# Starting place of the high weight copies in four buffers: 128, 0, 512 and 144 bytes modulo 1024

## The reference, cut to what matters

```
def _swiglu(xn, w_gate, w_up, w_down):
    return (jax.nn.silu(xn @ w_gate) * (xn @ w_up)) @ w_down
...
h = xn @ w_in                     # conv mixer, 1024 x 3072, then @ w_out
qkv = xn @ w_qkv                  # attention, 1024 x 3072, then @ w_o
proj = h @ w_in                   # second stack's mixer, 1024 x 3600, then @ w_out
```

## Time and profile before

| what | value |
|---|---|
| median of three runs | 2063.25 us |
| profiled execution, first to last instruction | 2062.1 us |
| TensorE matmul busy | 2036.8 us (99%), 9974 records |
| TensorE weight load busy | 1704.7 us (83%) |
| VectorE busy | 1684.8 us (82%) |
| ScalarE busy | 1022.3 us (50%) |
| GpSimd busy | 112.4 us (5%) |
| mean granted TensorE clock | 0.999 of 2.4 GHz |

### The profile page before, as it was taken

How to read it: one execution, slowest core, us unless ns; L and a number is a source line. 1 busy time by engine, 2 the same in 40 slices (tenths; PEclk the granted TensorE clock), 3 DMA queues, 4 the chain that set the end, 5 groups by cost and what they waited for, 6 DMA issues and landing times.

```text
span 2062.1 us, 26087 instructions
## 1 busy us (share of the span) xinstructions
PE 2036.8 (99%) x9974; PEld 1704.7 (83%) x9974; DVE 1684.8 (82%) x2820; ACT 1022.3 (50%) x1216; POOL 112.4 (5%) x238
## 2 busy tenths in 40 slices
PE   8999999999999999999999999999999999999998
PEld 7888878888978888888888889788888888988887
DVE  6888888886579887888889886989888877788986
ACT  4554445444554444554454445765445444575442
POOL 0010010000010000000010000010001000001000
PEclk9999999999999999999999999999999999999999
DMA  8576655756446556565566656346656756535662
GB/s 272 176 237 228 196 173 197 219 196 207 149 144 216 192 184 204 184 214 194 192 212 215 195 183 203 115 154 216 200 185 210 227 188 194 181 112 185 193 195 91
DMA packets 291166, 393.22 MB, mean 191 GB/s; under 512 B 9941, under 2 KB 257061, under 8 KB 290914
## 3 DMA queue, kind: packets, MB, share of 16 engines
q1 hardware_dynamic: 284176, 368.16, 55.1%
q10 hardware_dynamic: 4034, 14.23, 2.1%
q0 software_dynamic: 2832, 9.17, 1.6%
HBM read 390.44 MB, written 2.12 MB: 190 GB/s over the span
## 4 chain that ended last, share of the span: by engine, by line
PE 90%; DVE 6%; ACT 1%; issue 1%; POOL 1%; DMA 0%; POOLq 0%; SPq 0%; ACTq 0%; DVEq 0%
PE psum L577 25%; PE psum L578 25%; PE psum L579 25%; PE psum L601 4%; PE psum L619 2%; PE psum L616 2%; PE psum L623 2%; PE psum L603 2%; DVE w_lo L1569 2%; PE psum L712 1%; DVE conv_tmp L1657 1%; ACT squares L1210 1%; DVE mqk L1657 1%; DVE Y L1596 0%; DVE X L2072 0%
## 5 line engine op out<-in xcount | busy, mean ns | idle before, releaser
L1569 DVE TENSOR_TENSOR w_lo<-raw,w_hi 128x2048 fp32r<-128x2048 f32 x349 | 794.7, 2289 | 137.6 <-ACT w_hi L1184 134.7
L1184 ACT ACTIVATE w_hi<-raw 128x2048 fp32r<-128x2048 f32 x349 | 662.9, 1909 | 115.5 <-PE psum L579 83.3
L577 PE MATMUL psum<-w_hi,xT 128*128 128x512 f32 (+1 forms) x1424 | 552.3, 388 | 1.0 <-DVE xT L1754 1.0
L579 PE MATMUL psum<-w_hi,xT 128*128 128x512 f32 (+1 forms) x1424 | 549.0, 386 | 0.0
L578 PE MATMUL psum<-w_lo,xT 128*128 128x512 f32 (+1 forms) x1424 | 549.0, 386 | 0.0
L1620 DVE STREAM_TRANSPOSE h_turned<-h_full 32x128 f32<-32x128 f32 x1408 | 426.2, 303 | 21.1
L577 PEld LDWEIGHTS psum<-w_hi,xT 128*128 128x128 f32 x1424 | 267.4, 188 | 57.7 <-issue 2.9
L579 PEld LDWEIGHTS psum<-w_hi,xT 128*128 128x128 f32 x1424 | 267.4, 188 | 53.7
L578 PEld LDWEIGHTS psum<-w_lo,xT 128*128 128x128 f32 x1424 | 267.4, 188 | 53.3
L577 PE MATMUL psum<-w_hi,h_hi 128*128 128x512 f32 x768 | 299.5, 390 | 0.0
L579 PE MATMUL psum<-w_hi,h_lo 128*128 128x512 f32 x768 | 298.9, 389 | 0.0
(11 more groups left out here) (241 smaller groups left out, 1958.5 us busy)
## 6 DMA issues: line engine op xcount, KB each, us to landing
raw<-in_ffn_w_in SPq DMA_DIRECT2D x176, 512.0 KB, 4.9
raw<-in_ffn_w_gate SPq DMA_DIRECT2D x88, 512.0 KB, 4.0
raw<-in_ffn_w_up SPq DMA_DIRECT2D x88, 512.0 KB, 5.0
raw<-in_ffn_w_down SPq DMA_DIRECT2D x44, 1024.0 KB, 4.9
raw<-in_ffn_w_out SPq DMA_DIRECT2D x44, 1024.0 KB, 4.9
raw<-in_conv_w_in SPq DMA_DIRECT2D x20, 1024.0 KB, 5.6
raw<-in_mix_w_in SPq DMA_DIRECT2D x16, 1024.0 KB, 5.3
raw<-in_mix_w_in SPq DMA_DIRECT2D x24, 512.0 KB, 4.8
```

The costliest lines, as they stand in the source:

```text
L577: pe.matmul(dst, l_hi, r_hi, start=first, stop=False, skip_group_check=loose)
L579: return pe.matmul(dst, l_lo, r_hi, start=False, stop=last, skip_group_check=loose)
L1184: return act.activation(dst, source, ACT.Copy, **kw)
L1569: dve.tensor_tensor(w_lo[u % LO_RING][:], raw[u % LO_RING][:], f32(high(u)), ALU.subtract).then_inc(lo_ready, 1)
```

## The change

`high(u)` takes its offset from the buffer alone. The offsets are 0, 224, 96 and 4 elements, that is 0, 896, 384 and 16 bytes, so that every unit in buffers 0, 1, 2 and 3 begins at 128, 0, 512 and 144 bytes modulo 1024. The fifth buffer keeps 128. The plan of shifted units goes. No instruction, wait, transfer or buffer is added, removed or moved.

```diff
-ASIDE = 16
-NARROW = {"conv": (2, 3, 4, 5, 6, 7, 8, 9, 10, 12), "attn": tuple(range(2, 12)), "mix": tuple(range(2, 10)), "pool": (0,)}
+ASIDE = (0, 224, 96, 4)
...
-def plan_narrow(stages):
-
-    return {st["u0"] + n for st in stages for n in NARROW.get(st["kind"], ())}
...
-    narrow = plan_narrow(stages)
...
         def high(u):
-            off = ASIDE if hi_slot[u] < HI_RING and u in narrow else 0
+            off = ASIDE[hi_slot[u]] if hi_slot[u] < HI_RING else 0
             return w_hi[hi_slot[u]][:, off:off + UNIT]
```

## The result

The changed kernel takes 2080.01 us (median of four runs, 2079.72 to 2080.31), the kernel before in the same comparison 2063.09 us (2062.82 to 2063.88). The ratio is 1.008, with a 95% interval of 1.0068 to 1.0093: it is slower by 16.9 us. The profiled execution spans 2078.5 us (2062.1 before), at a mean granted clock of 0.998 of 2.4 GHz (0.999 before), so the clock is not the cause; a run of the changed kernel at 1.000 takes 2079.72 us.

The account below looks back on a forecast made before the run. TensorE matmul, busy 99%, was taken as the bound, so time is the sum of distances between its starts. 2062.1 + 13.6 + 0.8 = 2076.5 us, plus 1.15 to the median: 2077.7, given as 2077; 8 in 10: 2056 to 2096.

Parts of the forecast that it names:

- part 1: Long units in buffers 1, 2 and 3: 2960 steps with high weights moving leave their floor by 4.6 ns each, +13.6 us.
- the case of better places: Rival: the new places part two reads that meet in short and wide steps, -5.6 us, 2058 us; chance 0.16.
- restart row: Eight long steps after a restart in the earlier trace, 0.2313 us each, 4.6 ns above the floor; taken as the price.
- the wide row: A 512-column pass in a wide unit, 14 ns above the floor; upper bound for long steps, +41 us.
- Part 2: Short units: seven in buffer 0 go from 192 to 128, +0.8 us; nineteen in the other buffers taken as 0.
- Part 3: Wide units: 15 shifted ones, 16 pairs each, no order by address, taken as 0; bounds -3.4 and +3.4 us.
- Part 4: ScalarE and VectorE touching the high part at its new place: taken as 0; 3.2 us if VectorE slowed 2% without cover.
- The floor holds: Rival: long steps stay at 0.2267 us, as a 512-column step could hide any hold-up of the load; 2064 us, chance 0.34.
- only the 16-byte start hurts: Rival: only buffer 3's 976 matmuls lose 4.6 ns each, +4.5 us; 2069 us, chance 0.06, counted on the forecast's side.

Follow-up runs that it names:

- e1_long: Against the kernel before, only the 302 long units take the new places; the 41 shifted short and wide units stay at 192: 2079.21 us, ratio 1.0076.
- m2_small: Against the kernel before, high weights of long units begin 4, 16, 32 and 48 bytes past 128 in buffers 0 to 3: 2096.19 us, ratio 1.016.
- e2_short: Against the kernel before, only the 41 shifted short and wide units take the new places; long units stay at 128: 2063.51 us, ratio 1.0001.
- e7_buffer1: Against the kernel before, only long units in buffer 1 move, from 128 to 0: 2069.28 us, ratio 1.0027.
- e5_streams: Against the kernel before, all weights begin at 128, xT and h tiles at 256 (out_hi at 512), no unit shifted: 2102.51 us, ratio 1.019.
- e4_no_shift: Against the kernel before, no unit is shifted, all high parts begin at 128: 2065.31 us, ratio 1.001.
- e8_buffer3: Against the kernel before, only long units in buffer 3 move, from 128 to 144: 2071.52 us, ratio 1.0039.

## Why the prediction was right, step by step

The forecast of 2077 us and its main mechanism held: part 1, long steps that leave their floor because the two places are no longer a multiple of 256 bytes apart, was said to be the loss, and e1_long shows it alone. The size was in part luck, as the first two points say. (The sum of 2077.7 rounds to 2078 and not to 2077. And the case of better places needs (4.1 + 0.8) of its 6.4 us in short and wide units, over three quarters of them and not two thirds, before it can be told from none, since buffer 0's 0.8 us goes against it.)

- **Part 1.** Said: 2960 high-moving steps x 4.6 ns = 13.6 us. The steady patterns give 1984 steps x 3.33 = 6.6 us in buffers 1 and 2, and 6.67 per high step in buffer 3, 976 x 6.67 = 6.5: 13.1 together. So the sum held, but as a mean of two prices, 3.33 and 6.67 ns, one below the restart row's and one above. That the row's 4.6 lies near their mean of 4.4 is luck, for it measured something else. Its eight steps take 229, 233, 236, 224, 231, 236, 228 and 233 ns: they are a stream at distance 0 on its way back to the floor, the same steps as at the head of buffer 4, and no stream that stays off it. The price hangs on the distance besides: the 4 bytes of m2_small add 27 to 33 ns in three steps, 13 to 17 per high step, on either side of the 14 that I took from the wide row as the upper bound.
- **What was missed in part 1.** I said that buffers 0 and 4 would stay at 4.08 us for 18 steps and low-weight steps would stay. From the eleventh step on a unit in buffer 4 does; its head loses 0.04 us behind buffer 3. These heads are the 1.4 and 2.1 us of buffers 0 and 4, 3.5 us that had no term; the forecast is 2.9 us below the measured time. The 18 steps in buffers 1 and 2 take 4.11 us and not 4.14. In buffer 3 the low steps slow down as well, to 230 ns from 227, though their own operands didn't move. A step is not priced by its own addresses alone.
- **Part 2.** Buffer 0's short units went to 0.1200 as said. The units in the other buffers gave neither the 3.9 us gain nor a loss that can be measured (e2_short, 1.0001).
- **Part 3.** Zero was right, -0.4 us in the records. The reason given, no order by address, was half of it: there is an inherited pattern.
- **Part 4.** Copies at 1907 and 2291 ns against 1907 and 2290: nothing, as said.
- **The rivals.** "The floor holds" falls by the stretch at 136.90, "the new places are better" by e2_short, and "only the 16-byte start hurts" by e7_buffer1, where a start at 0 costs 5.65 us alone. The argument for the first was that a 512-column step would hide any hold-up of the load beside it. In e5_streams the place of the loaded operand makes 512-column steps longer, so it isn't hidden.
- **The two rules.** By the Trainium skill, "TensorE: Matmul & The Clock Gate", Part 2, the load beside a matmul takes no bandwidth from it. The prediction drew from it that the places could not matter. The runs decide against that: with the same data and the same instructions, e5_streams takes 39.1 us more (1.9 of them for the missing 64-byte shift) for the distance between the two operands. By the Trainium skill, "SBUF — State Buffer", section 'SBUF: two separate sides', SBUF has lines of 16 bytes, and accesses within one line have full bandwidth. That a start on a whole line would be enough was the prediction's reading, and the runs don't bear it out: 16, 32, 64 and 128 bytes are all whole lines, and all cost.

What stays open: which hardware makes the conflict. That it hangs on the distance is shown; that it is a meeting of two reads in the memory is an inference from that, and whether the load that runs beside the matmul matters or the matmul's own stationary slice was not told apart, as both lie at the same distance. Also open are the sizes in the table, and why the floor itself, 226.7 ns, stands above the 213.3 of 512 columns at 2.4 GHz; the ratio is 17/16, and no place tried went below it in a long unit. Distances to `out_hi` were not tried by themselves.

## What to carry to other kernels

Where float32r weights stream in steps of 512 columns while another tile is loaded as stationary operand, keep the starts of the two equal modulo 256 bytes, padding the tiles if need be; the other distances tried lengthened the steps by 1 to 5%. This doesn't carry over to steps of 256 columns, which were 0.120 us at equal places and 0.118 at 64 bytes (e4_no_shift against the kernel before). Moving everything together by 128 bytes cost nothing in long units, so look at differences of addresses and not at addresses. When TensorE is busy all the time, read the distance between starts over whole units, and look at the unit behind the changed one as well.

## What was not expected of the hardware

- A disturbed stream finds back to its floor by a path that repeats. In e8_buffer3 the steps behind buffer 3 take 229, 233, 236, 224, 231, 236, 228, 233, 230 ns and then 227, 227, 226 again and again. The kernel before takes the same steps, to 1 ns, at eleven places, each behind a step of 307 to 335 ns; the earlier trace rows is one. Behind buffer 1 of e7_buffer1 the path is another, 234, 229, 231, 231, 236, 228, 233, 230. Each costs some 40 ns, so a break in TensorE's stream costs a little more than its own length.
- A shift of 4 bytes is the dearest, 27 to 33 ns in three steps, and 128 the cheapest off the grid, 6.7.
- Patterns of wide units persist: 340 and 350 ns a pair at one and the same distance, depending, it seems, on what came before.
